# The first stage of a one-core transformer kernel: first norm with the tokens on the partitions, start-up transfers reordered, indexer's key and head weights in one product

## The reference

```python
def _rms_norm(x, gain):
    xf = x.astype(jnp.float32)
    xf = xf * lax.rsqrt(jnp.mean(xf * xf, axis=-1, keepdims=True) + NORM_EPS)
    return xf.astype(x.dtype) * gain
...
    hn = _rms_norm(x, norm_mix_pre[layer])
    ...
    proj = h @ w_in          # columns: q, k, v, q_idx (1024), k_idx (64), w_idx (16), 3 x 512 gates
    q_idx = _partial_rope(q_idx.reshape(bsz, s, IDX_HEADS, IDX_DIM), cos, sin)
    k_idx = _partial_rope(k_idx[:, :, None, :], cos, sin)[:, :, 0, :]
    w_idx = w_idx.astype(jnp.float32) * (IDX_HEADS ** -0.5 * IDX_DIM ** -0.5)
    ...
        rel = jax.nn.relu(jnp.einsum('bqhd,bsd->bqhs', qib, k_idx).astype(jnp.float32))
        score = jnp.einsum('bqhs,bqh->bqs', rel, wib)
        score = jnp.where(causal[None], score, -jnp.inf)
        _, sel = lax.top_k(score, top_k)
```

## Time and profile before

| | |
|---|---|
| three runs | 3947.86, 3943.45 and 6026.5 us; median 3947.86 us |
| profiled execution | 3948.83 us |
| its span, first to last instruction | 3947.2 us |
| TensorE busy, mean granted clock | 94% of the span, 0.973 of full speed |
| VectorE, ScalarE, GpSimd busy | 47%, 30%, 4% |
| HBM traffic | 62 GB/s over the span |

### The profile page before, as it was taken

The page is one execution under the profiler, slowest core; times in us unless marked ns, Lnnn a source line. Parts: engine busy times, 40 slices in busy tenths (PEclk is TensorE's granted clock), DMA queues, the critical chain, the costliest instruction groups (busy, mean ns, idle before and its releaser), DMA issues.

```text
span 3947.2 us, 45687 instructions
## 1 busy us (share of the span) xinstructions
PE 3701.5 (94%) x16746; PEld 2363.9 (60%) x16746; DVE 1839.8 (47%) x3679; ACT 1184.8 (30%) x2200; POOL 142.6 (4%) x227
## 2 busy tenths in 40 slices
PE   5999899998889999989999999998898999999989
PEld 2445488883445888756666666665554555555544
DVE  3744363644554636434545454544115555555541
ACT  1213210102342101124444444444003444445430
POOL 6600000000000000000000000000000000000000
PEclk8998999999999999999999999998899999999999
DMA  7531333431013333411010101110111122122111
GB/s 150 143 80 49 86 107 86 107 95 47 18 48 96 96 99 94 124 38 38 27 37 27 37 29 35 32 32 22 32 53 54 54 58 58 53 58 58 53 32 53
DMA packets 456578, 246.42 MB, mean 62 GB/s; under 512 B 44272, under 2 KB 448496, under 8 KB 456464
## 3 DMA queue, kind: packets, MB, share of 16 engines
q1 hardware_dynamic: 420528, 216.28, 20.0%
q0 software_dynamic: 14144, 28.36, 2.6%
q10 hardware_dynamic: 21792, 0.22, 0.5%
HBM read 229.96 MB, written 14.80 MB: 62 GB/s over the span
## 4 chain that ended last, share of the span: by engine, by line
PE 87%; DVE 5%; ACT 4%; issue 2%; ACTq 1%; DMA 0%; DVEq 0%; SPq 0%
PE bank L471 19%; PE bank L1193 15%; PE bank L1736 13%; PE bank L333 10%; PE bank L1722 4%; PE bank L1041 3%; PE bank L1105 3%; PE bank L1758 2%; PE bank L868 2%; PE bank L1086 2%; PE bank L1704 2%; PE bank L851 1%; PE bank L1746 1%; PE bank L1350 1%; DVE rs L290 1%
## 5 line engine op out<-in xcount | busy, mean ns | idle before, releaser
L1193 PE MATMUL bank<-hT,ring 128*128 128x512 f32 (+1 forms) x1664 | 632.7, 530 | 12.8 <-ACT hT L1610 6.0
L1736 PE MATMUL bank<-hT,ring 128*128 128x512 f32 x1504 | 510.1, 491 | 1.0 <-ACT arena L1926 1.0
L1193 PEld LDWEIGHTS bank<-hT,ring 128*128 128x128 f32 x1664 | 310.5, 191 | 289.6 <-issue 277.4
L1736 PEld LDWEIGHTS bank<-hT,ring 128*128 128x128 f32 x1504 | 278.4, 190 | 218.6 <-issue 204.7
L333 PE MATMUL bank<-big,ring 128*128 128x512 f32 (+1 forms) x1024 | 391.1, 545 | 5.3 <-ACTq L354 2.2
L333 PEld LDWEIGHTS bank<-big,ring 128*128 128x128 f32 x1024 | 196.4, 192 | 198.5 <-issue 185.1
L1093 ACT ACTIVATE arena<-bank 128x512 f32<-128x512 f32 (+2 forms) x224 | 118.4, 528 | 462.0 <-PE bank L1086 461.8
L471 PE MATMUL bank<-big,arena 128*128 128x256 f32 x1024 | 228.8, 379 | 0.0
L471 PEld LDWEIGHTS bank<-big,arena 128*128 128x128 f32 x1024 | 194.6, 190 | 26.5
L1061 DVE CUSTOM_DVE_ANT_0 arena<-bank,big 128x512 f32<-128x512 f32 (+2 forms) x152 | 101.3, 666 | 202.1 <-PE bank L1041 202.1
L1953 DVE TENSOR_REDUCE cols<-bank 128x1 f32<-128x768 f32 x128 | 116.5, 952 | 152.4 <-PE bank L1704 152.3
(11 more groups left out here) (309 smaller groups left out, 5114.2 us busy)
## 6 DMA issues: line engine op xcount, KB each, us to landing
ring<-in_mlp_w SPq DMA_DIRECT2D x128, 512.0 KB, 5.6
ring<-in_a_w_in SPq DMA_DIRECT2D x64, 512.0 KB, 4.0
ring<-in_b_w_in SPq DMA_DIRECT2D x64, 512.0 KB, 4.1
ring<-in_mod_w SPq DMA_DIRECT2D x48, 512.0 KB, 4.2
ring<-in_even_w_in SPq DMA_DIRECT2D x32, 512.0 KB, 4.0
bias_d<-tb POOLq DMA_DIRECT2D x96, 128.0 KB, 3.5
big<-bias_d POOLq DMA_DIRECT2D x16, 768.0 KB, 5.4
ring<-in_a_w_out SPq DMA_DIRECT2D x16, 512.0 KB, 4.0
```

The costliest lines, as they stand in the source:

```text
L1193: mm = pe.matmul(bk(b + n)[0:m, 0:z - a], ring[s][:, k, 0:m], (rhs or hcol)(k, a, z), start=k == 0, stop=k == kt - 1)
L1736: mm = pe.matmul(flatb[2][:, a:z], ring[s][:, k, :], hT[:, k, a:z], start=k == 0, stop=k == KT - 1)
```

## The change

- x comes in four transfers of 128 tokens, each with its own semaphore. The positions are issued ahead of them on SP. The constants move to ACT's queue, with the one gain vector that the first norm needs behind them.
- The first norm is taken from `xin`, the raw tile with tokens on the partitions: ACT squares a tile of 128 x 1024 and adds it up along the row (`accum_out`), takes the root of that one column; DVE takes the reciprocal and scales the tile into `xn`. TensorE transposes `xn`, ACT copies it out of the bank with the gain as scale into `hT`. `pe_sum`, `act_squares`, `act_std`, `dve_rs` and `dve_scaled` are no longer called for this norm; the engines bump their semaphores by hand.
- Key and head weights of the indexer are one slab of 80 columns and one product of eight steps into bank 7, interleaved with the transposes of `xn`.
- The transposes of raw x for `xT` are still done: five groups ahead of that, seven behind it, through banks 2 to 6; the copies to `xT` now stand in `dve_index` behind the key's copy.
- The context goes behind the first qi slab, the other 21 small transfers go to SP's queue behind the fourth qi slab, the four for the second block behind the fifth. DVE's wait for the small ones stands ahead of `dve_topk`.
- The key's rotation and the head weights' transposes are done behind the first query product; scores wait for them ahead of the second slab's.
- Three semaphores serve twice (`x_t`, `x_ev`, `o_d` in the output stage, the tables' in the second layer), with counts moved along.

```diff
@@ -144,7 +144,7 @@
 
         before, used = {}, [0] * SLOTS
         for phase, slots, times in (
-                ("kw", range(2), 1), ("qi", range(4), 2), ("gate", range(4), 3),
+                ("kw", range(1), 1), ("qi", range(4), 2), ("gate", range(4), 3),
                 ("att0", (0, 1, 2, 4, 5, 6), 2), ("wout0", range(8), 1),
                 ("mod0", range(8), 1),
                 ("up0a", range(8), 2), ("modx0", range(4), 1), ("down0a", range(8), 2), ("mody0", range(4, 8), 1),
...
@@ -203,52 +203,111 @@
             consume(n - 1, 1)
 
 
-        x_t, x_ev = sem("x_t"), sem("x_ev")
+        x_t, x_ev, o_d = sem("x_t"), sem("x_ev"), sem("o_d")
         xin = flat[:, 0:4 * DM].rearrange("p (t n) -> p t n", t=4)
         cin = flat[:, 4 * DM:6 * DM].rearrange("p (t n) -> p t n", t=2)
 
+
+
+        xt_in = [x_in] + [sem(f"xt_in{t}") for t in range(1, 4)]
+        x_sd, x_xn = sem("first_sd"), sem("first_xn")
+        xn = flat[:, 6 * DM:10 * DM].rearrange("p (t n) -> p t n", t=4)
+        x_stat = cols[:, 32:44].rearrange("p (a t) -> p a t", a=3)
+
         def sp_start(sp):
-            sp.dma_start(xin, d["x"][0].rearrange("(t p) n -> p t n", p=P)).then_inc(x_in, 16)
-            sp.dma_start(cst[:, :], d["consts"][:, 0:C_AX]).then_inc(const_in, 16)
-            sp.dma_start(cin, d["ctx_2"][0].rearrange("(t p) n -> p t n", p=P)).then_inc(x_in, 16)
-
-        def act_start(act):
+            for t in range(4):
+                sp.dma_start(xin[:, t, :], d["x"][0][P * t:P * t + P, :]).then_inc(xt_in[t], 16)
+
+        def sp_context(sp):
+            sp.dma_start(cin, d["ctx_2"][0].rearrange("(t p) n -> p t n", p=P)).then_inc(o_d, 16)
+
+        def sp_small(sp):
 
             with nc.allow_non_contiguous_dma(reason="small per-feature columns"):
                 for n, name in enumerate(("norm_mix_pre", "norm_mix_post", "norm_ffn_pre", "norm_ffn_post",
                                           "norm_g_2")):
                     for layer in range(2):
-                        act.dma_start(gains[:, 2 * n + layer, :], d[name][layer].rearrange("(k p) -> p k", p=P))\
-                            .then_inc(small_in, 16)
-                act.dma_start(cols[:, 0:3], d["odd_q_norm"][0].rearrange("(k p) -> p k", p=P)).then_inc(small_in, 16)
-                act.dma_start(cols[:, 3:5], d["odd_kv_norm"][0].rearrange("(k p) -> p k", p=P)).then_inc(small_in, 16)
+                        if n or layer:
+                            sp.dma_start(gains[:, 2 * n + layer, :], d[name][layer].rearrange("(k p) -> p k", p=P))\
+                                .then_inc(small_in, 16)
+                sp.dma_start(cols[:, 0:3], d["odd_q_norm"][0].rearrange("(k p) -> p k", p=P)).then_inc(small_in, 16)
+                sp.dma_start(cols[:, 3:5], d["odd_kv_norm"][0].rearrange("(k p) -> p k", p=P)).then_inc(small_in, 16)
                 for b in range(2):
                     for n, name in enumerate(("a_qn_g_2", "a_kn_g_2", "b_qn_g_2", "b_kn_g_2")):
-                        act.dma_start(cols[64 * b:64 * b + 64, 5 + n:6 + n],
-                                      d[name][0].rearrange("(p a) -> p a", a=1)).then_inc(small_in, 16)
-                act.dma_start(cols[:, 9:10], d["a_subln_g_2"][0].rearrange("(p a) -> p a", a=1)).then_inc(small_in, 16)
-                act.dma_start(cols[:, 12:24].rearrange("p (w f) -> p w f", w=3),
-                              d["even_conv_w"][0].rearrange("w (f p) -> p w f", p=P)).then_inc(small_in, 16)
-        SMALL = 16 * (10 + 2 + 8 + 2)
+                        sp.dma_start(cols[64 * b:64 * b + 64, 5 + n:6 + n],
+                                     d[name][0].rearrange("(p a) -> p a", a=1)).then_inc(small_in, 16)
+                sp.dma_start(cols[:, 9:10], d["a_subln_g_2"][0].rearrange("(p a) -> p a", a=1)).then_inc(small_in, 16)
+                sp.dma_start(cols[:, 12:24].rearrange("p (w f) -> p w f", w=3),
+                             d["even_conv_w"][0].rearrange("w (f p) -> p w f", p=P)).then_inc(small_in, 16)
+        SMALL = 16 * (9 + 2 + 8 + 2)
+
+        def act_start(act):
+            act.dma_start(cst[:, :], d["consts"][:, 0:C_AX]).then_inc(const_in, 16)
+            with nc.allow_non_contiguous_dma(reason="small per-feature columns"):
+                act.dma_start(gains[:, 0, :], d["norm_mix_pre"][0].rearrange("(k p) -> p k", p=P)).then_inc(tab0.pos_in, 16)
+            act.wait_ge(const_in, 16)
+            act.activation(x_stat[:, 2, 0:1], eps, ACT.Sqrt)
+            for t in range(4):
+                act.wait_ge(xt_in[t], 16)
+                act.activation(part(DM * t, DM), xin[:, t, :], ACT.Square, accum_out=x_stat[:, 0, t:t + 1])\
+                    .then_inc(n_sq, 2)
+                act.wait_ge(n_sq, 2 * t + 2)
+                act.activation(x_stat[:, 1, t:t + 1], x_stat[:, 0, t:t + 1], ACT.Sqrt, scale=1.0 / DM, bias=eps)\
+                    .then_inc(x_sd, 1)
+            act.wait_ge(tab0.pos_in, 32)
+            for k in range(KT):
+                act.wait_ge(x_t, 5 + k + 1)
+                act.activation(hT[:, k, 0:S], bk(k % 2), ACT.Copy, scale=gains[:, 0, k:k + 1]).then_inc(n_out, 1)
+
+
+        def pe_raw(pe, g):
+
+            t, k = g // 2, 4 * (g % 2)
+            if t < 4:
+                pe.wait_ge(xt_in[t], 16)
+            else:
+                pe.wait_ge(o_d, 16)
+            if g >= 5:
+                pe.wait_ge(x_ev, g - 4)
+            src = xin[:, t, :] if t < 4 else cin[:, t - 4, :]
+            for j in range(4):
+                m = pe.transpose(bk(2 + g % 5)[:, P * j:P * j + P], src[:, P * (k + j):P * (k + j) + P], ident)
+            m.then_inc(x_t, 1)
 
         def pe_start(pe):
             pe.wait_ge(const_in, 16)
-            pe.wait_ge(x_in, 32)
+            for g in range(5):
+                pe_raw(pe, g)
+            pe.wait_ge(x_xn, 8)
+            for k in range(KT + 1):
+                if k < KT:
+                    if k >= 2:
+                        pe.wait_ge(n_out, k - 1)
+                    for t in range(4):
+                        m = pe.transpose(bk(k % 2)[:, P * t:P * t + P], xn[:, t, P * k:P * k + P], ident)
+                    m.then_inc(x_t, 1)
+                if k > 0:
+                    if k == 1:
+                        arrived(pe, "kw", 0, 0)
+                    pe.wait_ge(n_out, k)
+                    m = pe.matmul(bk(7)[0:80, :], ring[0][:, k - 1, 0:80], hT[:, k - 1, 0:S], start=k == 1, stop=k == KT)
+            m.then_inc(slab_done[0], 1)
+            for g in range(5, 12):
+                pe_raw(pe, g)
+
+        def dve_start(dve):
+            for t in range(4):
+                dve.wait_ge(x_sd, t + 1)
+                dve.reciprocal(x_stat[:, 2, t:t + 1], x_stat[:, 1, t:t + 1]).then_inc(x_xn, 1)
+                dve.wait_ge(x_xn, 2 * t + 1)
+                dve.tensor_scalar(xn[:, t, :], xin[:, t, :], x_stat[:, 2, t:t + 1], None, ALU.mult).then_inc(x_xn, 1)
+
+        def dve_raw(dve):
             for g in range(12):
                 t, k = g // 2, 4 * (g % 2)
-                if g >= 4:
-                    pe.wait_ge(x_ev, g - 3)
-                src = xin[:, t, :] if t < 4 else cin[:, t - 4, :]
-                for j in range(4):
-                    m = pe.transpose(bk(g % 4)[:, P * j:P * j + P], src[:, P * (k + j):P * (k + j) + P], ident)
-                m.then_inc(x_t, 1)
-
-        def dve_start(dve):
-            for g in range(12):
-                t, k = g // 2, 4 * (g % 2)
-                dve.wait_ge(x_t, g + 1)
+                dve.wait_ge(x_t, g + 1 if g < 5 else KT + g + 1)
                 dve.tensor_copy(xT[:, k:k + 4, P * t:P * t + P],
-                                bk(g % 4).rearrange("p (j n) -> p j n", j=4)).then_inc(x_ev, 1)
+                                bk(2 + g % 5).rearrange("p (j n) -> p j n", j=4)).then_inc(x_ev, 1)
 
 
 
...
@@ -802,38 +867,32 @@
         ig_ev = sem("ig_ev")
 
         def sp_index(sp):
-            load(sp, "kw", 0, 0, w_in[:, :, O_KI:O_KI + 64], ring[0][:, :, 0:64])
-            load(sp, "kw", 1, 0, w_in[:, :, O_WI:O_WI + 16], ring[1][:, :, 0:16])
+            load(sp, "kw", 0, 0, w_in[:, :, O_KI:O_KI + 80], ring[0][:, :, 0:80])
 
             for j in range(8):
+                if j == 1:
+                    sp_context(sp)
+                if j == 4:
+                    sp_small(sp)
                 load(sp, "qi", j % 4, j // 4, w_in[:, :, O_QI + j * P:O_QI + j * P + P])
+                if j == 4:
+                    sp_mod_in(sp)
 
             def body(i):
                 for s in range(4):
                     load(sp, "gate", s, i, w_in[:, :, bass.ds(i * 512 + (O_G + s * P), P)])
             loop(sp, 0, 3, body)
 
-        def pe_index(pe, nm):
-
-            for k in range(KT):
-                pe.wait_ge(n_out, nm.k + k + 1)
-                if k == 0:
-                    arrived(pe, "kw", 0, 0)
-                m = pe.matmul(bk(0)[0:64, :], ring[0][:, k, 0:64], hT[:, k, 0:S], start=k == 0, stop=k == KT - 1)
```

(97 more changed lines are left out.)

12 lines of the change are left out of this document (5 added, 7 removed).

## The result

| | before | changed |
|---|---|---|
| median | 3947.86 us | 3925.8 us (3921.13 to 3926.16, 5 runs) |
| profiled execution, span | 3948.83, 3947.2 us | 3926.16, 3924.5 us |

The ratio of the times, changed to before, is 0.9947, with a 95% interval of 0.9936 to 0.9959. The kernel became faster by 22 us, where 37 were forecast; the time lies 0.8 us above the forecast range. (One run of before, at 6026.5 us, was a disturbed one and is left out of the ratio.)

The account below looks back on a forecast made before the run. The start was taken as bound by ACT's queue issuing 26 small transfers, then PE. Moving the second query product from 84.45 to 46.9 us saves 37.5: 3948.8 - 37.5 = 3911.3 us, own range 3907 to 3916, whole range 3902 to 3925.

Parts of the forecast that it names:

- Raw x: Transposes of raw x: five groups hidden in PE's wait, seven behind the loop on the path, ending at 35.0; 5.7 us given back.
- SP's queue: Small transfers on SP ahead of the fifth query slab: loads drain to about 24, small ones end at 42, no cost.
- every phase behind shifted by the same 37: Behind the second query product: all later work is unchanged and starts 37 us earlier.
- the slower rival: Small transfers on SP hold back the fifth query slab, 78 us late at 6 us an issue; 3949 to 3990 us, chance 0.03.
- the statistics: First norm on ACT, per tile: square 1.1 us, root 0.2, sum readout 0.19; 1.6 us with semaphore steps.
- first tile of x: Arrival of the first of x's four transfers, near 8.4 us on the trace's clock.
- xn ready: End of the first norm, x scaled by DVE: 16.0 us, bounds 13.5 and 18.
- interleaved loop ends: Transposes of xn interleaved with the 80-column product on PE end at 29.3 us, bounds 27.0 and 37.
- raw groups end: Last of the seven groups of raw x transposes behind the loop ends at 35.0 us.
- second product: Start of the second query product on PE, moved from 84.45 to 46.9 us.
- given back later: Later phases start earlier against POOL's transfers, slabs 1 to 2 us late in several phases; 3920 to 3945 us, chance 0.06.
- Late or slow loop: Interleaved loop held at the lower clock, or gain and slab landing at 20; 3914 to 3922 us, chance 0.20.

Follow-up runs that it names:

- run 1: The changed kernel with the context's transfer issued on SP ahead of the first query slab; 3911.83 us, ratio 0.9917.
- run 2: The changed kernel with the key and head-weight slab in ring place 7 instead of 0; 3913.44 us, ratio 0.992.
- run 5: The changed kernel with eight idle products, results never read, in the wait for the context; 3916.61 us, ratio 0.993.
- run 4: The kernel before with only the small transfers moved from ACT's queue to SP's; 3928.59 us, ratio 0.9962.
- run 7: The kernel before with small transfers on SP and key and head weights in one 80-column product, old norm; 3930.7 us, ratio 0.9962.
- run 8: The kernel of run 7 with the 80-column slab in ring place 7, still the old norm; 3925.58 us, ratio 0.9957.
- run 3: The kernel of run 2 with the key's rotation moved right behind the 80-column product, ahead of seven raw groups; 3908.34 us, ratio 0.9905.
- run 6: The changed kernel with 64 idle transposes in the wait for the context; 3919.95 us, ratio 0.9938.

## Why the prediction was wrong

**The step that failed** is in the paragraph "Raw x": "The context, issued behind the first query slab, is then far in", and its twin in "SP's queue", "the queue first drains six loads ... to about 24". I took SP's list of transfers as a list that only bandwidth delays. The first query slab's `load` waits for ring place 0, and the key slab is in it. Before, that wait stood in front of nothing that was urgent: x, constants and context were issued ahead of it. The change put the context behind it. I had the count of descriptors and the drain rate, and never asked which of the six loads waits on a semaphore; the prediction names such a wait for the fifth slab and none for the first. Runs 1 and 2 show it from two sides: either moving the context ahead of the wait or taking the wait away brings the second product to 47.8 and 48.1, against my 46.9.

The 11.2 us of the miss are: 9.2 at the raw groups (they ended at 44.2, forecast 35.0), of which run 5 shows 1.7 to be the lower clock; 0.2 at the first product (7.23 for 6.97); and 1.7 from its end to the second product, 6.62 for 4.9, of which 1.0 is the lower clock's rotation (2.08 for 1.12) and the rest a copy of the key that took 1.30 instead of 0.45. That copy ran beside an addition of GpSimd (53.67 to 54.93); in runs 1, 2 and 5, clear of one, it took 0.42. Whether the one slows the other was not tested.

A second step failed too, "every phase behind shifted by the same 37". The 26.4 us at the second product were 22.7 at the end, and these 3.7 and the 11.2 are together the 14.9 us by which the profiled execution (3926.16) missed 3911.3. They are followed below.

Two small slips of the working change nothing: six products and five groups of transposes from 21.8 end at 29.1, not 29.3, and the slower rival eats up the saving from 4.1 us an issue on, not 4.2.

**What held.** Terms on either side of that step came out close:

| term | forecast | measured |
|---|---|---|
| first tile of x | 8.4 | 9.4 |
| xn ready | 16.0 | 16.05 |
| interleaved loop ends | 29.3 | 29.13 |
| raw groups end, context early (run 1) | 35.0 | 34.8 |
| second product, context early (run 1) | 46.9 | 47.8 |
| small issues on SP | 0.83 us each | 19.8 us for 21, 0.94 each |

The agreement for xn is luck of signs: the first tile came 1.0 us later than forecast, and ACT, which set the pace as forecast, took 1.37 us a tile from 9.47 on where I had 1.6 from 8.4 on. Of the statistics, these rows of the changed kernel, by line and shape, stand against 1.1, 0.2 and 0.19:

```profile
L252 ACT ACTIVATE arena<-big 128x1024 f32<-128x1024 f32 x4 | 4.2, 1046 | 2.4 <-DMA big<-in_x 2.4
...
L255 ACT ACTIVATE cols<-cols,cst 128x1 f32<-128x1 f32 x4 | 1.2, 295 | 0.1
L252 ACT ACTIVATION_READ_ACCUMULATOR arena<-big 128x1 f32 x4 | 0.7, 186 | 0.0
```

**The rivals.** The time, 3925.8, lay in the band of "given back later" (3920 to 3945), but its mechanism did not happen: no slab was late, and PE has no wait for a transfer behind 40.5. What was lost behind the second product is told below. "Late or slow loop" did not happen either, the clock was at 1.00 from 22 us. The slower rival's price (6 us an issue) was far off at 0.94. It named the right queue, though, and the wrong transfer in it.

**Where the whole change's gain comes from**, by the second product: small transfers off ACT, 18.5 us (run 4); one product, 3.3, and 0.9 more with a place of its own (runs 7 and 8); the new norm together with the new order of x, constants, context and key rotation, 13.6 (run 8 against run 2); together 36.3, to 48.1. As submitted, 10.0 of these were lost with SP's wait.

**From the second product to the end** the shift is not constant, though the code there is the same in all kernels. VectorE's instructions are the same ones from there on, so they can be paired from the last one backwards. The table has how much earlier than before they start, in us, in the profiled executions; the places are times of before:

| | second product | at 188 | at 888 | at 1082 | at 3801 | last |
|---|---|---|---|---|---|---|
| changed | 26.4 | 23.8 | 23.2 | 22.9 | 22.7 | 22.7 |
| run 1 | 36.7 | 36.9 | 36.0 | 36.1 | 36.0 | 37.1 |
| run 4 | 18.5 | 18.3 | 16.4 | 19.1 | 18.6 | 22.6 |
| run 5 | 30.8 | 29.9 | 28.6 | 31.2 | 31.2 | 32.3 |
| run 7 | 21.9 | 23.0 | 22.8 | 22.8 | 22.0 | 18.8 |

The changed kernel lost its 3.7 us early: 2.0 by the third product (8.82 for 6.87, the lower clock), and the rest nearly all by 888. Nothing changes in its long middle. Other kernels gained or lost 1 to 4 us at two places, from 888 to 1082 and behind 3801. In the second TensorE idles often, and the granted clock differs there. The same stretch of the code in the kernel before, in run 7 and in run 4:

```profile
3790.00:3810.00 20.00, 13.86 (x92) 0.71 0.10 27
3810.00:3830.00 20.00, 14.23 (x93) 0.87 0.00 1
```

```profile
3770.00:3790.00 20.00, 14.17 (x92) 0.66 0.10 27
3790.00:3810.00 20.00, 14.34 (x80) 0.66 0.00 1
```

```profile
3770.00:3790.00 20.00, 14.40 (x98) 0.83 0.10 27
3790.00:3810.00 20.00, 13.85 (x97) 1.00 0.00 1
```

What sets the clock there was not tried and stays open. It is not the edit, or not the edit alone: of the nine runs of before beside run 1, two took 3939.1 and 3939.4 us at a mean granted clock of 0.977, and seven 3945.7 to 3947.8 at 0.973 or 0.974. Against the runs of before on the same chip the medians shifted by 35.5, 33.9, 39.0 and 18.8 us (runs 1 to 4) and by 29.4, 26.0, 15.3, 21.0 and 36.7 (runs 5 to 9), where the second product had shifted by 36.7, 36.4, 40.8 and 18.5, and by 30.8, 29.7, 21.9, 22.8 and 40.8. So I trust the start of that product more than the median for what a part is worth, and the median alone for what the whole gains.

## What to carry to other kernels

When a transfer is moved in a queue, write down for each entry ahead of it the semaphore that it waits for and when that comes, before its bandwidth; a ring place shared by the first two users is such a wait. A product that is removed may have covered a transfer that its neighbour released (run 7). Removing a wait uncovers the one behind it: run 8 won 0.9 us of the 3.0. Measure a part of a start-up by the start of the first common instruction behind it, since the total carries a few us of clock from stages that the edit never touched.

## What the hardware showed that was not expected

- A gap of 2.3 us in TensorE, the wait for VectorE behind the key's rotation in run 2, was followed by 0.58 of the full clock from 46 to 50 us; in run 1 the same gap of 2.3 us was followed by 1.00. With a gap of 0.4 us (run 3) it stayed at 1.00. What decides it is open.
- In run 2 the profile gives a granted clock of 1.00 from 16 to 20 us, although the first two matmuls of the 80-column product took 1.97 us there and later ones 0.86. So early in a trace the duration is the safer witness.
- Transposes alone kept the granted clock at 1.00 for 9 us (run 6).
- VectorE's copy of the key took 1.30 us beside an addition of GpSimd and 0.42 clear of one (changed kernel against runs 1, 2 and 5).
- Issuing three slabs on SP held its queue for 10.03 us (3.3 each) while the DMA engines were busy throughout, and the 21 small transfers for 0.94 each.
- The constants landed 6.0 us after their issue on ACT's queue beside x on SP's, against 10.3 behind x on one queue.
